# Slot weights as one-hot products in fp32r, weight split in two parts on the moving side

## Chip, cores and metric

The kernel runs on one core of a Trainium2 chip. The metric is the device time in microseconds (us) of one execution; lower is better. The time of the kernel before is the median of three runs.

## What is computed

One transformer layer over 512 latent tokens (two token mixers, a merge, then a PEER feed-forward part and a final norm). Only the PEER part matters here. For each token and each of 8 heads, 16 of 128 x 128 = 16384 single-neuron experts are chosen, so a token has 128 slots, each with an expert number and a softmax weight:

```python
idx = (jnp.take_along_axis(i1, ci // PEER_TOPK, axis=-1) * N_KEYS
       + jnp.take_along_axis(i2, ci % PEER_TOPK, axis=-1)).reshape(PEER_BLOCK, -1)
g = jax.nn.softmax(sc, axis=-1).reshape(PEER_BLOCK, -1)
act = jax.nn.gelu(jnp.einsum("med,md->me", u[idx], hb), approximate=False)
return jnp.einsum("me,med->md", (g * act).astype(hb.dtype), v[idx])
```

The kernel does not gather. It computes the activation of all 16384 experts for all tokens, and needs beside it a dense matrix W(i, j) per token: the sum of the weights of the slots whose expert is (i, j). With the 128 slots of a token on the partitions, W is a product of two one-hot matrices, one for i and one for j, with the weight multiplied into one of them.

## The kernel before

The part after the merge has three phases. `phase_route` chooses the experts. `phase_weights` builds W for 512 tokens and stores it to DRAM. `phase_experts` reads it back, multiplies it with the activations and forms the output. Through all three runs `Hidden`, the product of the expert matrix u with the tokens, in 128 tiles of 128 experts. Each tile is 8 times `product`: three fp32r matmuls of a 128x128 stationary operand and 512 moving columns (high*high, low*high, high*low; L85, L86, L87), 24 matmuls in all. ScalarE applies gelu to the tile (L1889) and splits the high part of a coming u tile (L1869, `Hidden.split`); then `Hidden.rest` (L1873) subtracts it to get the low part, on GpSimd in the route phase and on VectorE in the weights phase; SyncE loads u and stores activations.

`phase_weights` is the phase that the change touches. It has 64 steps (16 loop bodies with 4 steps). In each step every engine does one tile of `Hidden` and two groups of four tokens (`SUB = 4`). A group uses one of four buffers (`S = 4`), so a buffer is used again two steps later. The order on the engines within step q is fixed by the program:

- TensorE: the 24 matmuls of the tile, then for each of the two groups the wait for its operands and four fp32 matmuls `ps_w <- oi, oj` (L2368), stationary operand `oi` (128x128), 128 moving columns of `oj`. I call these two groups the slot section of the step, s the first and s' the second.
- VectorE: for each of the two groups, `oi` of tokens 0 and 1 (two tensor_scalar, is_equal and times weight, L2322) and `oj` of all four tokens (one tensor_tensor with both inputs broadcast, L2324); then `Hidden.rest` of the step. What it builds in step q+1 is what TensorE uses in step q+1, so these operations stand behind `rest` of step q.
- ScalarE: gelu, split, and for each group `away` = |i - iota| (L2377), the evacuation of `ps_w` to `w_block` (L2400) and `oi` of token 2 as relu(w - w*away) (L2381), one turn ahead.
- GpSimd: for each group a small copy (L2343) and `oi` of token 3 (L2349).

`slots` holds for all tokens i, j, weight, -i and -weight; it is written at the end of `phase_route` (L2236 to L2240). After every 64 tokens SyncE stores 4 MB of W to DRAM (L2306).

Of the kernel before, what the change touches and what calls it, by code (L numbers as in the profile page):

```python
# [13 lines left out]
F32R = mybir.dt.float32r  # L14
U32 = mybir.dt.uint32
ALU = mybir.AluOpType
ACT = mybir.ActivationFunctionType
AX = mybir.AxisListType

P = 128  # L20
D = 1024
KT = D // P
TX, TC = 512, 256
# [19 lines left out]
PH, NK, TOPK = 8, 128, 16  # L43
# [1858 lines left out]
def phase_route(nc, a, b, hidden):  # L1902


    with ExitStack() as ctx:
        sb = alloc(nc, ctx)

        def sem(name):
# [7 lines left out]
        S = b.acc[:, 4:8].rearrange("p (h k) (t n) -> p h k t n", h=2, n=NK)  # L1916
# [12 lines left out]
        iota = sb("iota16", [P, TOPK])  # L1929
        src = sb("slot_src", [P, 2, TT, PH, TOPK])  # L1930
        SC = sb("SC", [P, TT, PH, TOPK])
        weight = sb("slot_weight", [P, TT, PH * TOPK])
        total = sb("soft_total", [P, TT * PH])
        ps_q = [ctx.enter_context(nc.psum_tensor(f"ps_q{k}", [P, TX], F32)) for k in range(2)]
        ps_s = [ctx.enter_context(nc.psum_tensor(f"ps_sc{k}", [P, TT, NK], F32)) for k in range(2)]
        keys_in, iota_in = sem("rt_keys"), sem("rt_iota")
# [13 lines left out]
        turn, turn_g = sem("rt_turn"), sem("rt_turn_pool")  # L1950
        sub_done, exp_done, soft, weight_done, turned, slots_out = (
            sem(f"sl_{n}") for n in ("sub", "exp", "dve", "weight", "turned", "out"))
# [167 lines left out]
        def _(v):  # L2120
# [12 lines left out]
            with v.Fori(0, PH // 2) as i:  # L2133
                for hh in range(2):
# [3 lines left out]
                    for t, p in both:  # L2138
                        m = v.max(top[:, hh, t, p, 0:8], S[:, hh, p, t, :])
                    dve_s.mark(m)  # L2140
                for hh in range(2):
                    when(i, f"max1{hh}")
                    for t, p in both:
                        m = v.max_index(ix[:, hh, t, p, 0:8], top[:, hh, t, p, 0:8], S[:, hh, p, t, :])
                    dve_s.mark(m)
                    for t, p in both:
                        m = v.match_replace(left[:, hh, t, p], top[:, hh, t, p, 0:8], S[:, hh, p, t, :], LOW)
                    dve_s.mark(m)
                for hh in range(2):
                    when(i, f"left{hh}", s_free[hh])  # L2150
                    for t, p in both:
                        m = v.max(top[:, hh, t, p, 8:16], left[:, hh, t, p])
                    dve_s.mark(m)
                for hh in range(2):
                    when(i, f"max2{hh}")
                    for t, p in both:
                        m = v.max_index(ix[:, hh, t, p, 8:16], top[:, hh, t, p, 8:16], left[:, hh, t, p])
                    dve_s.mark(m)

                    for t in range(TT):  # L2160
                        m = v.tensor_tensor(cand[:, hh, t], top[:, hh, t, 0, :].unsqueeze(2).to_broadcast([P, TOPK, TOPK]),
                                            top[:, hh, t, 1, :].unsqueeze(1).to_broadcast([P, TOPK, TOPK]), ALU.add)
                    dve_s.mark(m)
                flat = cand[:].rearrange("p h t a c -> p h t (a c)")
                for hh in range(2):
                    when(i, f"cand{hh}")
                    for t in range(TT):
                        m = v.max(ctop[:, hh, t, 0:8], flat[:, hh, t])
# [60 lines left out]
            link = Count(v, soft)  # L2229
# [5 lines left out]
            for k in range(3):  # L2235
                v.wait_ge(turned, k + 1)  # L2236
                bank = ps_q[k][:] if k < 2 else ps_s[0][:].rearrange("p t n -> p (t n)")
                v.tensor_copy(b.slots[:, k, 0:TX], bank).then_inc(slots_out, 1)
                if k != 1:
                    v.tensor_scalar(b.slots[:, 3 + k // 2, 0:TX], bank, -1.0, None, ALU.mult).then_inc(slots_out, 1)  # L2240


W_TOKENS = 64
# [3 lines left out]
def phase_weights(nc, a, b, hidden, w_dram):  # L2247
# [6 lines left out]
    with ExitStack() as ctx:  # L2254
        sb = alloc(nc, ctx)

        def sem(name):
            return b.semaphore(nc, name)


        oi = b.acc[:, 0:S].rearrange("p s (k n) -> p s k n", n=NK)
        oj = b.acc[:, S:2 * S].rearrange("p s (k n) -> p s k n", n=NK)
        iota = sb("iota128", [P, NK])[:]
        away = sb("w_away", [P, S, NK])
        cur = sb("w_token", [P, S, 2])
        wb = sb("w_block", [P, 2, NK, W_TOKENS])
        ps = [ctx.enter_context(nc.psum_tensor(f"ps_w{k}", [P, SUB, NK], F32)) for k in range(S)]
        small_in = sem("w_in")
        built, built_a, mm, evac = ([sem(f"w_{n}{k}") for k in range(S)] for n in ("built", "built_act", "mm", "evac"))
        dist = sem("w_dist")  # L2270
        built_p, fetched, turn = sem("w_built_pool"), sem("w_fetched"), sem("w_turn")
        stored = [sem(f"w_stored{k}") for k in range(2)]
        block = ctx.enter_context(nc.Block())
        n_outer = W_BLOCKS // 2
# [37 lines left out]
        @block.vector  # L2312
        def _(v):
            v.wait_ge(small_in, 16)

            def body(t0, n, half, g, o):
                for q in range(steps):
                    for s, r, dt in subs(q):

                        v.wait_ge(mm[s], n * TURNS + (r + 1))  # L2320
                        for k in range(SUB - 2):
                            v.tensor_scalar(oi[:, s, k], iota, b.slots[:, 0, bass.ds(t0 + (dt + k), 1)],  # L2322
                                            b.slots[:, 2, bass.ds(t0 + (dt + k), 1)], ALU.is_equal, ALU.mult)
                        v.tensor_tensor(oj[:, s], iota.unsqueeze(1).to_broadcast([P, SUB, NK]),  # L2324
                                        b.slots[:, 1, bass.ds(t0 + dt, SUB)].unsqueeze(2).to_broadcast([P, SUB, NK]),
                                        ALU.is_equal).then_inc(built[s], 1)
                    hidden.rest(v, n + (ROUTE_T + 1), q)

            bodies(v, body)

        @block.gpsimd
        def _(g_):

            g_.wait_ge(small_in, 16)
            g_.sem_inc(built_p, S)

            def body(t0, n, half, g, o):
                for q in range(steps):
                    for s, r, dt in subs(q):

                        g_.wait_ge(built_p, n * (TURNS * S) + (r * S + s + 1))
                        g_.sem_inc(turn, 1)
                        g_.tensor_copy(cur[:, s], b.slots[:, 0:3:2, bass.ds(t0 + (dt + SUB - 1), 1)].rearrange(  # L2343
                            "p k o -> p (k o)")).then_inc(fetched, 1)
                        g_.wait_ge(fetched, n * (TURNS * S) + (r * S + s + 1))

                        g_.wait_ge(mm[s], n * TURNS + (r + 1))
                        g_.sem_inc(turn, 1)
                        g_.tensor_scalar(oi[:, s, SUB - 1], iota, cur[:, s, 0:1], cur[:, s, 1:2],  # L2349
                                         ALU.is_equal, ALU.mult).then_inc(built_p, 1)  # L2350

            bodies(g_, body)

        @block.tensor
        def _(pe):
            for s in range(S):
                pe.sem_inc(mm[s], 1)

            def body(t0, n, half, g, o):
                for q in range(steps):  # L2360
                    hidden.multiply(pe, n + ROUTE_T, q)
                    for s, r, dt in subs(q):
                        pe.wait_ge(built[s], n * TURNS + (r + 1))
                        pe.wait_ge(built_a[s], n * TURNS + (r + 1))
                        pe.wait_ge(built_p, n * (TURNS * S) + (r * S + s + S + 1))
                        pe.wait_ge(evac[s], n * TURNS + (r + 1))
                        for k in range(SUB):
                            m = pe.matmul(ps[s][:, k, :], oi[:, s, k], oj[:, s, k], start=True, stop=True)  # L2368
                        m.then_inc(mm[s], 1)

            bodies(pe, body)

        @block.scalar
        def _(act):

            def measure(t, s):
                act.activation(away[:, s], iota, ACT.Abs, bias=b.slots[:, 3, bass.ds(t, 1)]).then_inc(dist, 1)  # L2377

            def build(t, s, turn_):
                act.wait_ge(dist, turn_ * S + (s + 1))  # L2380
                act.activation(oi[:, s, SUB - 2], away[:, s], ACT.Relu, bias=b.slots[:, 2, bass.ds(t, 1)],  # L2381
                               scale=b.slots[:, 4, bass.ds(t, 1)]).then_inc(built_a[s], 1)

            act.wait_ge(small_in, 16)
            for s in range(S):
                act.sem_inc(evac[s], 1)
                measure(s * SUB + (SUB - 2), s)
                build(s * SUB + (SUB - 2), s, 0)

            def body(t0, n, half, g, o):  # L2390
                for q in range(steps):
                    hidden.gelu(act, n + ROUTE_T, q)
                    hidden.split(act, n + (ROUTE_T + 1), q)
                    for s, r, dt in subs(q):
                        t_next = t0 + (S * SUB + dt + SUB - 2)
                        measure(t_next, s)
                        act.wait_ge(mm[s], n * TURNS + (r + 2))

                        act.wait_ge(stored[half], o * 16 + 16)
                        act.activation(wb[:, half, :, bass.ds(g * BODY + dt, SUB)].rearrange("p j t -> p t j"),  # L2400
                                       ps[s][:], ACT.Copy).then_inc(evac[s], 1)
                        build(t_next, s, n * TURNS + (r + 1))

            bodies(act, body)


# [183 lines left out]
def build_program(nc, a, out):  # L2590
    with ExitStack() as ctx:
# [67 lines left out]
        with ExitStack() as route:  # L2659
            st = alloc(nc, route)  # L2660

            b.slots = st("slots", [P, 5, TX + 16])
            phase_route(nc, a, b, hidden)
            phase_weights(nc, a, b, hidden, w_dram)
        b.clear_semaphores(nc)
# [92 lines left out]
```

## Time and profile before

| | us |
|---|---|
| median of 3 runs | 2840.35 (2839.32 to 2850.03) |
| the profiled execution | 2841.56 |
| its span, first to last instruction | 2839.3 |
| TensorE busy, whole span | 2548.7 (90%) |
| route phase's last 100 us, TensorE busy | 68.9 of 100 |
| weights phase, 1420 to 1886, TensorE busy | 464.1 of 466 |
| the same stretch, VectorE, ScalarE, GpSimd busy | 221.8, 297.2, 238.3 |
| from 1950 to the end, TensorE busy | 875.4 of 889 |

The page gives each engine's busy share; the table cuts the span at the phases, since the phases have different limits. A matmul's duration in the trace holds its way through the array, so matmuls overlap, and the pace is read from start to start.

### The profile page before, as it was taken

The numbers are of one execution on the slowest core, as the hardware profiler recorded it, in microseconds if no ns is written. First come the engines' busy times: TensorE is split into PE (matmuls) and PEld (weight loads), VectorE is DVE, ScalarE is ACT, GpSimd is POOL, SyncE is SP. The second block draws the span as 40 slices with busy tenths as digits, with TensorE's granted clock in tenths as the row PEclk, the third lists the DMA queues.
The fourth block names the chain that finished last, engine by engine and source line by source line (L and its number), as shares of the span: only waits on it lengthen the run. The fifth ranks groups of instructions, "written<-read, shape, count | busy, mean of one in ns | idle before, by whom it ended". The sixth has DMA issues, their size and how long they took to land. (4 is left out here: it accounts for less than half of the span.)

```text
span 2839.3 us, 53307 instructions
## 1 busy us (share of the span) xinstructions
PE 2548.7 (90%) x19772; PEld 2098.7 (74%) x19772; DVE 1327.9 (47%) x2679; ACT 1026.1 (36%) x1763; POOL 767.5 (27%) x627
## 2 busy tenths in 40 slices
PE   5998839759995997899599999979999999999998
PEld 2884429559983875788488888868888888888886
DVE  4764345465554232499744444420014444444443
ACT  3322433423333222332266666642223222222222
POOL 1520013124422342554455555524420000000000
PEclk9999759979997998999799999989999999999999
DMA  5551000000003221422335444554436555555551
GB/s 226 184 170 37 1 8 1 9 2 0 0 5 111 88 97 33 160 92 82 107 141 184 167 169 182 214 200 145 144 118 234 188 198 187 201 184 203 182 204 60
DMA packets 164052, 349.10 MB, mean 123 GB/s; under 512 B 13512, under 2 KB 79560, under 8 KB 161936
## 3 DMA queue, kind: packets, MB, share of 16 engines
q1 hardware_dynamic: 163984, 348.19, 35.2%
q8 instruction: 44, 0.72, 0.1%
q14 instruction: 24, 0.20, 0.0%
HBM read 276.84 MB, written 71.30 MB: 123 GB/s over the span
## 5 line engine op out<-in xcount | busy, mean ns | idle before, releaser
L85 PE MATMUL ps_a<-h_hi,u_hi 128*128 128x512 f32 x1024 | 407.3, 398 | 23.5 <-PEq L105 16.5
L2537 DVE TENSOR_TENSOR v_lo<-v_raw,v_hi 128x1024 fp32r<-128x1024 f32 x128 | 158.2, 1236 | 564.9 <-ACT v_hi L2495 564.9
L86 PE MATMUL ps_a<-h_hi,u_lo 128*128 128x512 f32 x1024 | 401.1, 392 | 0.0
L87 PE MATMUL ps_a<-h_lo,u_hi 128*128 128x512 f32 x1024 | 400.9, 391 | 0.0
L2495 ACT ACTIVATE v_hi<-v_raw 128x1024 fp32r<-128x1024 f32 x128 | 135.8, 1061 | 477.7 <-PE ps_a L87 469.3
L85 PE MATMUL ps_y<-gated_hi,v_hi 128*128 128x512 f32 x768 | 299.5, 390 | 3.1 <-DVE gated_lo L2539 3.1
L86 PE MATMUL ps_y<-gated_hi,v_lo 128*128 128x512 f32 x768 | 299.5, 390 | 0.0
L87 PE MATMUL ps_y<-gated_lo,v_hi 128*128 128x512 f32 x768 | 299.3, 390 | 0.0
L85 PEld LDWEIGHTS ps_a<-h_hi,u_hi 128*128 128x128 f32 x1024 | 194.3, 190 | 62.6 <-issue 23.1
L87 PEld LDWEIGHTS ps_a<-h_lo,u_hi 128*128 128x128 f32 x1024 | 193.6, 189 | 40.8
L1889 ACT ACTIVATE act<-ps_a 128x512 f32<-128x512 f32 x128 | 76.4, 597 | 407.6 <-PE ps_a L87 407.6
L86 PEld LDWEIGHTS ps_a<-h_hi,u_lo 128*128 128x128 f32 x1024 | 194.0, 189 | 38.0
L2349 POOL TENSOR_SCALAR mixed<-iota,w_token 128x128 f32<-128x128 f32 x128 | 149.5, 1168 | 213.3 <-PE ps_w L2368 197.8
L1873 POOL TENSOR_TENSOR u_lo<-u_raw,u_hi 128x1024 fp32r<-128x1024 f32 x64 | 154.8, 2422 | 188.7 <-ACT u_hi L1869 188.7
L1873 DVE TENSOR_TENSOR u_lo<-u_raw,u_hi 128x1024 fp32r<-128x1024 f32 x64 | 78.4, 1225 | 242.4 <-ACT u_hi L1869 242.4
L85 PEld LDWEIGHTS ps_y<-gated_hi,v_hi 128*128 128x128 f32 x768 | 144.5, 188 | 33.6 <-DVE v_lo L2537 3.5
L86 PEld LDWEIGHTS ps_y<-gated_hi,v_lo 128*128 128x128 f32 x768 | 144.6, 188 | 30.1
L87 PEld LDWEIGHTS ps_y<-gated_lo,v_hi 128*128 128x128 f32 x768 | 144.5, 188 | 30.1
L1869 ACT ACTIVATE u_hi<-u_raw 128x1024 fp32r<-128x1024 f32 x128 | 134.4, 1051 | 57.4 <-DMA u_raw<-in_uT 57.4
L2400 ACT ACTIVATE w_block<-ps_w 128x512 f32 x128 | 141.2, 1103 | 0.0
L1681 POOL TENSOR_TENSOR mg_w_lo<-mg_raw,mg_w_hi 128x1024 fp32r<-128x1024 f32 x36 | 87.7, 2437 | 196.7 <-ACT mg_w_hi L1730 196.7
L2368 PEld LDWEIGHTS ps_w<-mixed 128*128 128x128 f32 x1024 | 124.1, 191 | 5.0
(497 smaller groups left out, 5314.9 us busy)
## 6 DMA issues: line engine op xcount, KB each, us to landing
u_raw<-in_uT SPq DMA_DIRECT2D x128, 512.0 KB, 3.5
v_raw<-in_v SPq DMA_DIRECT2D x128, 512.0 KB, 4.9
a_scratch<-act SPq DMA_DIRECT2D x128, 256.0 KB, 2.2
w_scratch<-w_block SPq DMA_DIRECT2D x8, 4096.0 KB, 12.0
w_ring<-w_scratch SPq DMA_DIRECT2D x64, 512.0 KB, 4.5
gated<-a_scratch SPq DMA_DIRECT2D x128, 256.0 KB, 4.9
mg_raw<-in_w_merge SPq DMA_DIRECT2D x36, 512.0 KB, 3.4
vM<-in_ada_rows SPq DMA_DIRECT2D x32, 512.0 KB, 4.7
```

Of the source, the lines that this page charges most:

```text
L85: pe.matmul(out, wh, xh, start=first, stop=False)
L86: pe.matmul(out, wl, xh, start=False, stop=False)
L87: return pe.matmul(out, wh, xl, start=False, stop=last)
L1681: g.tensor_tensor(wl[:, k], raw[:, k], wh[:, k], ALU.subtract).then_inc(w_lo, 1)
L1869: act.activation(self.uh[:, q], self.raw[:, q % 2], ACT.Copy).then_inc(self.hi, 1)
L1873: eng.tensor_tensor(self.ul[:, q], self.raw[:, q % 2], self.uh[:, q], ALU.subtract).then_inc(self.lo, 1)
L1889: act.activation(self.act[:, q % 2], self.ps[q % 2][:], ACT.Gelu).then_inc(self.out, 1)
L2349: g_.tensor_scalar(oi[:, s, SUB - 1], iota, cur[:, s, 0:1], cur[:, s, 1:2], ALU.is_equal, ALU.mult).then_inc(built_p, 1)
L2368: m = pe.matmul(ps[s][:, k, :], oi[:, s, k], oj[:, s, k], start=True, stop=True)
L2400: act.activation(wb[:, half, :, bass.ds(g * BODY + dt, SUB)].rearrange("p j t -> p t j"), ps[s][:], ACT.Copy).then_inc(evac[s], 1)
L2495: act.activation(vh[:, q], v_raw[:, q], ACT.Copy).then_inc(v_hi, 1)
L2537: v.tensor_tensor(vl[:, q], v_raw[:, q], vh[:, q], ALU.subtract).then_inc(v_lo, 1)
```

## The change

In `phase_weights` all operands become fp32r. The weight is split in two fp32r parts, high and low (w = high + low), and multiplied into the j side, which is the moving one: `oh` = high * onehot(j), `ol` = low * onehot(j). The i side is a plain one-hot `oi`. A token is now two matmuls into the same PSUM columns instead of one: `oi` with `oh`, then `oi` with `ol`. Each operand is built for four tokens in one operation: VectorE writes `mark` = onehot(j) and `oi` (is_equal) and `oh` = mark * high; GpSimd writes `ol` = mark * low. The building on ScalarE and the small copies on GpSimd are gone. In `phase_route`, `slots` gets the rows i, j, high and low instead of five rows.

```diff
-                v.tensor_copy(b.slots[:, k, 0:TX], bank).then_inc(slots_out, 1)
-                if k != 1:
-                    v.tensor_scalar(b.slots[:, 3 + k // 2, 0:TX], bank, -1.0, None, ALU.mult).then_inc(slots_out, 1)
+                if k < 2:
+                    v.tensor_copy(b.slots[:, k, 0:TX], bank).then_inc(slots_out, 1)
+                else:
+                    link(v.tensor_scalar(w_high[:], bank, 1.0, None, ALU.mult))
+                    v.tensor_copy(b.slots[:, 2, 0:TX], w_high[:]).then_inc(slots_out, 1)
+                    v.tensor_tensor(b.slots[:, 3, 0:TX], bank, w_high[:], ALU.subtract).then_inc(slots_out, 1)
...
+            def spread(row, t):
+                return b.slots[:, row, bass.ds(t, SUB)].unsqueeze(2).to_broadcast([P, SUB, NK])
+
+            line = iota.unsqueeze(1).to_broadcast([P, SUB, NK])
...
+                        v.wait_ge(built_p[s], n * TURNS + (r + 1))
+                        v.tensor_tensor(mark[:, s], line, spread(1, t0 + dt), ALU.is_equal).then_inc(marked[s], 1)
                         v.wait_ge(mm[s], n * TURNS + (r + 1))
-                        for k in range(SUB - 2):
-                            v.tensor_scalar(oi[:, s, k], iota, b.slots[:, 0, bass.ds(t0 + (dt + k), 1)],
-                                            b.slots[:, 2, bass.ds(t0 + (dt + k), 1)], ALU.is_equal, ALU.mult)
-                        v.tensor_tensor(oj[:, s], iota.unsqueeze(1).to_broadcast([P, SUB, NK]),
-                                        b.slots[:, 1, bass.ds(t0 + dt, SUB)].unsqueeze(2).to_broadcast([P, SUB, NK]),
-                                        ALU.is_equal).then_inc(built[s], 1)
+                        v.tensor_tensor(oi[:, s], line, spread(0, t0 + dt), ALU.is_equal)
+                        v.wait_ge(marked[s], n * TURNS + (r + 1))
+                        v.tensor_tensor(oh[:, s], mark[:, s], spread(2, t0 + dt), ALU.mult).then_inc(built[s], 1)
                     hidden.rest(v, n + (ROUTE_T + 1), q)
...
-                        g_.tensor_copy(cur[:, s], b.slots[:, 0:3:2, bass.ds(t0 + (dt + SUB - 1), 1)].rearrange(
-                            "p k o -> p (k o)")).then_inc(fetched, 1)
...
-                        g_.tensor_scalar(oi[:, s, SUB - 1], iota, cur[:, s, 0:1], cur[:, s, 1:2],
-                                         ALU.is_equal, ALU.mult).then_inc(built_p, 1)
+                        g_.wait_ge(marked[s], n * TURNS + (r + 1))
                         g_.wait_ge(mm[s], n * TURNS + (r + 1))
+                        g_.tensor_tensor(ol[:, s], mark[:, s],
+                                         b.slots[:, 3, bass.ds(t0 + dt, SUB)].unsqueeze(2).to_broadcast([P, SUB, NK]),
+                                         ALU.mult).then_inc(built_p[s], 1)
...
                         for k in range(SUB):
-                            m = pe.matmul(ps[s][:, k, :], oi[:, s, k], oj[:, s, k], start=True, stop=True)
+                            pe.matmul(ps[s][:, k, :], oi[:, s, k], oh[:, s, k], start=True, stop=False)
+                            m = pe.matmul(ps[s][:, k, :], oi[:, s, k], ol[:, s, k], start=False, stop=True)
                         m.then_inc(mm[s], 1)
...
-                        t_next = t0 + (S * SUB + dt + SUB - 2)
-                        measure(t_next, s)
                         act.wait_ge(mm[s], n * TURNS + (r + 2))
...
-                        build(t_next, s, n * TURNS + (r + 1))
```

## Rows read from the trace of the kernel before

**Rows 1.** Busy time by stretch of all engines, then granted clock and DMA.
```profile
1420.00:1886.00 466.00, 464.14 (x2557) 403.02 (x2555) 221.76 (x448) 297.15 (x519) 238.26 (x256) 1.00 0.47 170
```

**Rows 2.** Groups by line, 1420 to 1886: busy, mean ns, idle before and releaser.
```profile
L2368 PE MATMUL ps_w<-mixed 128*128 128x128 f32 x1024 | 124.5, 275 | 0.0
L1873 DVE TENSOR_TENSOR u_lo<-u_raw,u_hi 128x1024 fp32r<-128x1024 f32 x64 | 78.4, 1225 | 242.4 <-ACT u_hi L1869 242.4
```

**Rows 3.** Timeline of one step: start, length (us), engine; x16 counts merged instructions.
```profile
1599.84 1.95 PE L2368 MATMUL ps_w<-mixed 128*128 128x128 f32 x16
...
1600.13 0.60 ACT L1889 ACTIVATE act<-ps_a 128x512 f32<-128x512 f32 x1 [2.72 <-PE ps_a L87]
...
1601.54 0.48 PE L85 MATMUL ps_a<-h_hi,u_hi 128*128 128x512 f32 x1
...
1601.70 1.23 DVE L1873 TENSOR_TENSOR u_lo<-u_raw,u_hi 128x1024 fp32r<-128x1024 f32 x1 [3.88 <-ACT u_hi L1869]
...
1602.84 0.60 DVE L2322 TENSOR_SCALAR mixed<-iota,slots 128x128 f32<-128x128 f32 x2
...
1603.21 1.59 POOL L2349 TENSOR_SCALAR mixed<-iota,w_token 128x128 f32<-128x128 f32 x1 [0.23 <-POOL w_token L2343]
...
1603.36 0.69 DVE L2324 TENSOR_TENSOR mixed<-iota,slots 128x512 f32<-128x512 f32 x1
...
1603.96 0.60 DVE L2322 TENSOR_SCALAR mixed<-iota,slots 128x128 f32<-128x128 f32 x2
...
1607.08 1.95 PE L2368 MATMUL ps_w<-mixed 128*128 128x128 f32 x16
...
1608.78 0.48 PE L85 MATMUL ps_a<-h_hi,u_hi 128*128 128x512 f32 x1
...
1608.85 1.22 DVE L1873 TENSOR_TENSOR u_lo<-u_raw,u_hi 128x1024 fp32r<-128x1024 f32 x1 [3.69 <-ACT u_hi L1869]
```

**Rows 4.** Weight loads (PEld), timeline and groups: 128 stationary columns, fp32, fp32r, transposes.
```profile
53.79 2.75 PEld L369 LDWEIGHTS ps_pc<-ident,fC 2*128 2x128 f32 x24 [1.61 <-ACT fC L267]
264.39 1.57 PEld L1202 LDWEIGHTS ps_gt<-gate_ident,gate_turn 36*128 36x128 f32 x24 [0.76 <-issue]
L2368 PEld LDWEIGHTS ps_w<-mixed 128*128 128x128 f32 x1024 | 124.1, 191 | 5.0
L85 PEld LDWEIGHTS ps_a<-h_hi,u_hi 128*128 128x128 f32 x1024 | 194.3, 190 | 62.6 <-issue 23.1
```

**Rows 5.** Timeline of fp32r matmuls with 256 moving columns, start to start.
```profile
150.49 0.28 PE L85 MATMUL ps_pc<-h_hi,win_hi 128*128 128x256 f32 x1
...
152.76 0.28 PE L87 MATMUL ps_pc<-h_lo,win_hi 128*128 128x256 f32 x1
```

**Rows 6.** Timeline where VectorE and GpSimd both run two-input operations.
```profile
363.11 2.48 POOL L1374 TENSOR_TENSOR mixed<-ml_hc,ml_ssq 128x512 f32<-128x512 f32 x2
363.25 1.44 DVE L1606 TENSOR_TENSOR mixed<-mixed 128x512 f32<-128x512 f32 x1 [1.00 <-POOL mixed L1374]
364.62 1.52 DVE L1603 TENSOR_TENSOR mixed<-ml_hc,ml_ssq 128x512 f32<-128x512 f32 x1
365.55 1.48 POOL L1374 TENSOR_TENSOR mixed<-ml_hc,ml_ssq 128x512 f32<-128x512 f32 x1
```

**Rows 7.** One line's instructions: ns min/median/max, then GpSimd groups of other sizes.
```profile
L1374 POOL TENSOR_TENSOR mixed<-ml_hc,ml_ssq x4: 1033/1482/1541, 361.6 to 365.6; 128x512 f32<-128x512 f32 x4
L1873 POOL TENSOR_TENSOR u_lo<-u_raw,u_hi 128x1024 fp32r<-128x1024 f32 x64 | 154.8, 2422 | 188.7 <-ACT u_hi L1869 188.7
L755 POOL TENSOR_TENSOR ks_x<-ke,ginv_x 128x256 f32<-128x256 f32 x16 | 11.6, 727 | 3.8 <-POOL qs_x L755 3.8
```

**Rows 8.** Timelines of the end of the route phase and of the weights phase.
```profile
1413.44 2.34 POOL L1873 TENSOR_TENSOR u_lo<-u_raw,u_hi 128x1024 fp32r<-128x1024 f32 x1 [3.05 <-ACT u_hi L1869]
1882.89 1.05 ACT L1869 ACTIVATE u_hi<-u_raw 128x1024 fp32r<-128x1024 f32 x1
1886.88 0.33 SPq L2306 DMA_DIRECT2D w_scratch<-w_block  x1
```

More of the change, by code:

```diff
@@ L1933, in phase_route @@
         total = sb("soft_total", [P, TT * PH])
+        w_high = sb("weight_hi", [P, TX], F32R)
         ps_q = [ctx.enter_context(nc.psum_tensor(f"ps_q{k}", [P, TX], F32)) for k in range(2)]
@@ L2258, in sem @@
             return b.semaphore(nc, name)
-        oi = b.acc[:, 0:S].rearrange("p s (k n) -> p s k n", n=NK)
-        oj = b.acc[:, S:2 * S].rearrange("p s (k n) -> p s k n", n=NK)
+        mark = b.acc[:, 0:S].rearrange("p s (k n) -> p s k n", n=NK)
+        oi, oh, ol = (sb(n, [P, S, SUB, NK], F32R) for n in ("one_i", "one_j_hi", "one_j_lo"))
         iota = sb("iota128", [P, NK])[:]
-        away = sb("w_away", [P, S, NK])
-        cur = sb("w_token", [P, S, 2])
         wb = sb("w_block", [P, 2, NK, W_TOKENS])
@@ L2268, in phase_weights @@
         small_in = sem("w_in")
-        built, built_a, mm, evac = ([sem(f"w_{n}{k}") for k in range(S)] for n in ("built", "built_act", "mm", "evac"))
-        dist = sem("w_dist")
-        built_p, fetched, turn = sem("w_built_pool"), sem("w_fetched"), sem("w_turn")
+        marked, built, built_p, mm, evac = ([sem(f"w_{n}{k}") for k in range(S)]
+                                            for n in ("marked", "built", "built_pool", "mm", "evac"))
         stored = [sem(f"w_stored{k}") for k in range(2)]
@@ L2332, in _ @@
         def _(g_):
-            g_.wait_ge(small_in, 16)
-            g_.sem_inc(built_p, S)
+            for s in range(S):
+                g_.sem_inc(built_p[s], 1)
             def body(t0, n, half, g, o):
@@ L2339, in body @@
                     for s, r, dt in subs(q):
-                        g_.wait_ge(built_p, n * (TURNS * S) + (r * S + s + 1))
-                        g_.sem_inc(turn, 1)
-                        g_.tensor_copy(cur[:, s], b.slots[:, 0:3:2, bass.ds(t0 + (dt + SUB - 1), 1)].rearrange(
-                            "p k o -> p (k o)")).then_inc(fetched, 1)
-                        g_.wait_ge(fetched, n * (TURNS * S) + (r * S + s + 1))
+                        g_.wait_ge(marked[s], n * TURNS + (r + 1))
                         g_.wait_ge(mm[s], n * TURNS + (r + 1))
-                        g_.sem_inc(turn, 1)
-                        g_.tensor_scalar(oi[:, s, SUB - 1], iota, cur[:, s, 0:1], cur[:, s, 1:2],
-                                         ALU.is_equal, ALU.mult).then_inc(built_p, 1)
+                        g_.tensor_tensor(ol[:, s], mark[:, s],
+                                         b.slots[:, 3, bass.ds(t0 + dt, SUB)].unsqueeze(2).to_broadcast([P, SUB, NK]),
+                                         ALU.mult).then_inc(built_p[s], 1)
             bodies(g_, body)
@@ L2363, in body @@
                         pe.wait_ge(built[s], n * TURNS + (r + 1))
-                        pe.wait_ge(built_a[s], n * TURNS + (r + 1))
-                        pe.wait_ge(built_p, n * (TURNS * S) + (r * S + s + S + 1))
+                        pe.wait_ge(built_p[s], n * TURNS + (r + 2))
                         pe.wait_ge(evac[s], n * TURNS + (r + 1))
                         for k in range(SUB):
-                            m = pe.matmul(ps[s][:, k, :], oi[:, s, k], oj[:, s, k], start=True, stop=True)
+                            pe.matmul(ps[s][:, k, :], oi[:, s, k], oh[:, s, k], start=True, stop=False)
+                            m = pe.matmul(ps[s][:, k, :], oi[:, s, k], ol[:, s, k], start=False, stop=True)
                         m.then_inc(mm[s], 1)
@@ L2374, in _ @@
         def _(act):
[L2376 to L2384, printed above, removed]
             for s in range(S):
                 act.sem_inc(evac[s], 1)
-                measure(s * SUB + (SUB - 2), s)
-                build(s * SUB + (SUB - 2), s, 0)
             def body(t0, n, half, g, o):
@@ L2660, in build_program @@
             st = alloc(nc, route)
-            b.slots = st("slots", [P, 5, TX + 16])
+            b.slots = st("slots", [P, 4, TX + 16])
             phase_route(nc, a, b, hidden)
```

## The prediction

> **What bounds the kernel now.** I read first the busy time cut by stretch, then the groups by line within the weights phase, then the timeline of one step. In the weights phase TensorE is busy 464.1 of 466 us at the full clock, and no other engine is over 64% [rows 1]. So this phase is bound by TensorE alone, and the reader should see that ScalarE, VectorE and GpSimd have slack. The slot matmuls start behind no idle time at all [rows 2]. In the timeline a slot section starts at 1599.84 and the next one at 1607.08: a step takes 7.24 us, and 64 of them are 463 us. Of these the slot section is 1607.08 to 1608.78, 1.70 us, and the tile of `Hidden` from 1601.54 to 1607.08, 5.54 us [rows 3]. Eight fp32 matmuls show as 16 records, so a record takes 106 ns.
>
> **What the change does to TensorE.** It takes away 16 records of fp32 (8 tokens) and puts 16 fp32r matmuls there (8 tokens, 2 each). The trace shows no fp32r matmul with 128 moving columns. Two bounds: fp32r with 256 columns goes from 150.49 to 152.76 in 20 steps from start to start, 113.5 ns each [rows 5], so the stream alone should need about half, 57 ns for 128 columns. But each matmul also loads 128 columns of weights. With only 2 moving columns, the 24 loads of L369 take 2.75 us: (2.75 - 0.19) / 23 = 111 ns from load to load; there the stream is nothing, so the load sets the pace. That is fp32. The load of an fp32r operand is 190 ns long in the trace, that of an fp32 operand 191 ns, whereas the transposes of L1202 have loads at (1.57 - 0.14) / 23 = 62 ns [rows 4]. So fp32r loads look like fp32 loads, not like those of the transposes. The two products of a token use the same `oi`, but the program gives each matmul its own load; I find no load left out in this trace. I take 16 x 107 = 1.71 us for the new slot section: TensorE gains nothing. Ends: 16 x 62 = 0.99 us below, and above 16 x 113 = 1.81 us (the pace of rows 5), or 3.40 us if a short fp32r matmul should pass four times like fp32.
>
> The Trainium skill (TensorE: Matmul & The Clock Gate, section LDWEIGHTS) gives a load as columns / 1.2, an estimate of 107 ns for 128 columns; rows 4 agree. The same page (section Back-to-back issue gap) gives about 81 ns for a load and matmul pair with 128 columns, and it says the fast weight load is off for FP32; by 81 ns the section would be an estimated 1.30 us. No row shows that pace with these operands; it is a rival below.
>
> **What it does to VectorE and GpSimd.** VectorE had per step four tensor_scalar (0.60 us a pair) and two tensor_tensor of 128x512, and `rest` [rows 3]. It now has six tensor_tensor of 128x512 with two SBUF inputs, 0.60 us from start to start, 0.68 from start to end (L2324 is just this form). 6 x 0.60 + 1.14 = 4.7 us of 7.24: enough room by count. GpSimd had a copy and a 128x128 operation, and now has one two-input operation of 128x512 per group. The nearest row is L1374, same size and same kind of broadcast: 1033 ns when alone. The other GpSimd operations of 256 and 1024 elements (727 and 2422 ns) would give 1.28 us for 512 [rows 7].
>
> The count is not enough, because of two things. First, where these operations stand. VectorE builds the operands of step q+1 behind `rest` of step q, and `rest` waits for ScalarE's split, which follows gelu, which follows the tile. With T the start of a slot section, `rest` starts at T+1.86 (1601.70 - 1599.84), and at T+1.77 in the next step (1608.85 - 1607.08), mean 1.81, and the next VectorE operation 1.14 later, at T+2.95 [rows 3]. Second, two-input operations of the two engines do not overlap. L1606 starts at 363.25 and takes 1.44 us in place of 0.69; it ends 0.58 us after the GpSimd operation (363.11 + 1.00 = 364.11) has ended. The GpSimd operation that waits meanwhile ends at 365.55, 0.9 us after L1606 at 364.69, and L1603 ends 0.59 after that, at 366.14 [rows 6]. They take turns, 0.9 us for GpSimd, 0.59 for VectorE. In the weights phase itself L2349 takes 1.59 us instead of 0.79 beside L2324 [rows 3].
>
> The Trainium skill (GPSIMD Engine Reference, section Specifications) says the same of the design: the SBUF interfaces are shared with VectorE, with contention for VectorE instructions with two SBUF inputs. It speaks against this change, and the trace agrees (1.44 us for 0.69).
>
> So from T, in the order of the queues: mark 2.95, oi 3.55 to 4.23; GpSimd's ol (waiting since mark ended at 3.63) to 5.13; oh to 5.72; mark' from 5.64, oi' 6.24 to 6.92; ol' to 7.82; oh' to 8.41. TensorE can start s' about 0.15 later (semaphore, and a load that isn't ahead), at T+8.56. With the old step it needs s' at T + 7.24 + 0.85 = T+8.09. It comes 0.47 us late. The group s is ready at 5.72, long before 7.24. Behind s' stand its matmuls, 0.85, and the next tile, 5.54, so the loop is T(q+2) = T(q) + 8.56 + 0.85 + 5.54 = 14.95 us, 7.475 per step instead of 7.24. The sum: 64 x 0.235 = +15.0 us. If GpSimd took turns in another order, the sum of the port's occupation is the same, so I take this as robust against the order. With the 1.28 us form GpSimd is 0.38 longer, twice in two steps: another 64 x 0.38 = +24 us. With a pace of 113 ns on TensorE: +0.05 per step, +3.
>
> **What it does elsewhere.** ScalarE loses away and build; it had slack (297 of 466) [rows 1], gelu and split come before them in its order, so this gives nothing in a step. At the end of the phase the last evacuation no longer stands behind one build and two measures. The split ends at 1883.94, two evacuations of about 1.1 would end at 1886.2, and the store that now starts at 1886.88 [rows 8] starts 0.7 us earlier: -0.7 us, since the next phase waits for the store. At the end of the route phase VectorE has three operations instead of two behind the last transpose, some 0.5 us more; it would end near 1414, and GpSimd's L1873 ends at 1415.78 in the same block [rows 8], which covers it. Without this cover it would cost 0.5. The waits that VectorE gets: for `built_p` of two steps ago, for `mm` of two steps ago, for `marked`, its own mark that ended during oi. The first two are fulfilled long before; behind the waiting instruction `rest` is queued, whose slack is T(q+1)+1.81 - (T(q)+8.41), over 0.8 us. SyncE's loads follow `rest`, as before. The phase of the experts is untouched.
>
> The sum is +15.0 - 0.7 = +14.3 on the profiled 2841.56, which is 1.2 over the median; on the median it is 2854.7, I say 2855.
>
> **Rivals.**
> 1. Contention does not bite (the engines share less than rows 6 show, or `ol` gets its turn in a gap). Then s' is ready at 2.95 + 5 x 0.60 + 0.68 = T+6.63, in time, and TensorE sets the step at 7.24 to 7.34: 2840 to 2846, not slower. For: VectorE's operations in rows 3 aren't longer beside GpSimd's. Against: rows 6. It decides as soon as s' comes before T+8.09.
> 2. The slot section shrinks to 0.99 us (loads like the transposes'). TensorE's step would be 6.53. With contention the loop is 8.56 + 0.49 + 5.54 = 14.59, 7.30 a step: +4, 2844, same. The chain eats the gain.
> 3. The same without contention: 64 x (6.53 - 7.24) = -45, 2795, faster. By the page's 81 ns it would be an estimated -26 us. This needs two things against the rows.
> 4. Short fp32r matmuls pass four times: section 3.40, step 8.94, +109 us, 2949. For: nothing under 256 columns is in the trace. Against: the 256-column ones pass once.
> That the change doesn't do what it says, that is, TensorE's slot section stays at 1.7 us, is part of my forecast and of rival 1.
>
> **How the numbers follow.** Chances: forecast 0.55 (2846 to 2880, 0.34 of it above 0.5%, as the unknown costs, GpSimd's above all, point upwards), rival 1 0.22, rival 2 0.06, rival 3 0.09, rival 4 0.08. A measurement can tell about 0.5% (14 us) from no change. Slower: 0.34 + 0.08 = 0.42. Same: 0.21 + 0.22 + 0.06 = 0.49. Faster: 0.09. The range leaves out rivals 3 and 4 and takes in GpSimd's upper bound: 2838 to 2880. The forecast's own range is 2846 to 2880.
>
> **What the profile after would show.** Slot section: 16 PE records of about 107 ns, 1.7 us; 62 ns would be rivals 2 and 3, 212 ns rival 4. VectorE: oh and oh' of about 1.5 us instead of 0.69, each beside a GpSimd operation; all at 0.69 would be rival 1. TensorE idle before s' of about 0.5 us every other step or 0.24 in each, with GpSimd or VectorE as the releaser; the step at 7.47. The forecast would be wrong if `rest` or the split move, if GpSimd takes another time than 0.9 to 1.3 us, or if the port is shared otherwise.

## The result and the profile after

The changed kernel takes 2853.24 us (median of 12 runs, 2849.54 to 2863.01), the kernel before beside it 2839.84 us (12 runs). The ratio is 1.0044, 95% interval 1.0029 to 1.0059: slower by 0.44%, which is 12.5 us (the two medians lie 13.4 us apart), clear of the noise, but under the 0.5% that I had set as the border between same and slower. The forecast was 2855.

Whole spans of single executions are a bad measure here. The profiled executions differ by 8.7 us (2839.3 and 2848.0), but in the one of after the weights phase already starts 5.2 us sooner (the load of iota is issued at 1411.62 instead of 1416.83), before any changed work. So I measure in the phase itself. The mean step is the distance from the first to the last slot section by 63:

| | first section | last section | mean step | iota load to first load of the next phase | rest |
|---|---|---|---|---|---|
| before | 1426.08 | 1882.20 | 7.240 | 483.5 | 939.0 |
| after | 1420.75 | 1890.84 | 7.462 | 497.7 | 938.7 |

The phase is 14.3 us longer, of which the steps are 63 x 0.222 = 14.0. The next phase takes the same time to 0.3 us. This step of after answers to [rows 3]; the columns are start, length, engine:

```profile
1601.64 2.06 ACT L2385 ACTIVATE w_block<-ps_w 128x512 f32 x2
1601.78 1.23 DVE L1873 TENSOR_TENSOR u_lo<-u_raw,u_hi 128x1024 fp32r<-128x1024 f32 x1 [1.21 <-ACT u_hi L1869]
1602.92 0.69 DVE L2327 TENSOR_TENSOR mixed<-iota,slots 128x512 f32<-128x512 f32 x1
...
1603.52 0.69 DVE L2329 TENSOR_TENSOR one_i<-iota,slots 128x512 fp32r<-128x512 f32 x1
1603.79 1.32 POOL L2346 TENSOR_TENSOR one_j_lo<-mixed,slots 128x512 fp32r<-128x512 f32 x1 [3.76 <-DVE mixed L2327]
1604.12 1.53 DVE L2331 TENSOR_TENSOR one_j_hi<-mixed,slots 128x512 fp32r<-128x512 f32 x1
1605.58 0.68 DVE L2327 TENSOR_TENSOR mixed<-iota,slots 128x512 f32<-128x512 f32 x1
1606.18 0.68 DVE L2329 TENSOR_TENSOR one_i<-iota,slots 128x512 fp32r<-128x512 f32 x1
1606.44 1.33 POOL L2346 TENSOR_TENSOR one_j_lo<-mixed,slots 128x512 fp32r<-128x512 f32 x1 [1.33 <-DVE mixed L2327]
1606.79 1.52 DVE L2331 TENSOR_TENSOR one_j_hi<-mixed,slots 128x512 fp32r<-128x512 f32 x1
...
1607.20 0.22 PE L2365 MATMUL ps_w<-one_j_hi,one_i 128*128 128x128 f32 x1
...
1607.37 0.27 PE L2365 MATMUL ps_w<-one_j_hi,one_i 128*128 128x128 f32 x1
...
1607.48 0.27 PE L2366 MATMUL ps_w<-one_j_lo,one_i 128*128 128x128 f32 x1
...
1608.37 0.33 PE L2365 MATMUL ps_w<-one_j_hi,one_i 128*128 128x128 f32 x1 [0.16 <-DVE one_j_hi L2331]
...
1614.82 0.22 PE L2365 MATMUL ps_w<-one_j_hi,one_i 128*128 128x128 f32 x1
```

Read it from the top: VectorE's subtraction (u_lo), then mark (its tile shares a buffer that the profile calls `mixed`), one_i, and then one_j_hi with 1.53 us where the same size takes 0.69 two lines above. It ends at 1605.65, 0.54 us after GpSimd's operation (1605.11), and the GpSimd operation takes 1.32 us because it stands still until one_i is through at 1604.21 and then needs 0.90. The same happens in the second group, whose one_j_hi ends at 1608.31; 0.06 later TensorE starts the group's first matmul, which had to wait. The slot section started at 1607.20, the next one at 1614.82: 7.62 us. The step before it took 7.29 (1599.91 to 1607.20). Late and timely steps alternate, 14.91 us for this pair, 14.92 in the mean. The groups by line over the phase show that this holds for all of them (idle before, and its releaser, at the end):

```profile
L2331 DVE TENSOR_TENSOR one_j_hi<-mixed,slots 128x512 fp32r<-128x512 f32 x127 | 193.9, 1527 | 0.0
L2327 DVE TENSOR_TENSOR mixed<-iota,slots 128x512 f32<-128x512 f32 x126 | 85.9, 682 | 0.0
L2329 DVE TENSOR_TENSOR one_i<-iota,slots 128x512 fp32r<-128x512 f32 x126 | 85.9, 682 | 0.0
L1873 DVE TENSOR_TENSOR u_lo<-u_raw,u_hi 128x1024 fp32r<-128x1024 f32 x64 | 78.4, 1225 | 60.8 <-ACT u_hi L1869 60.8
```

VectorE's idle time before u_lo fell from 242.4 us [rows 2] to 60.8. And TensorE waits for it, which it never did before; from the waits between 1430 and 1890 (total, times, longest):

```profile
PEld ps_w L2365 <- DVE one_j_hi L2331: 8.7, 30, 0.3
PE ps_w L2365 <- DVE one_j_hi L2331: 2.2, 14, 0.2
```

Thirty waits of the weight load, one in every other step. The 14 waits of the matmuls lie in the same delays, so the two sums are not to be added. What the lateness costs is read from the steps: the timely ones take 7.287 us, and over the phase the late ones bring the mean to 7.462, 63 x 0.175 = 11.0 us.

The other 3 us are in every step, 7.287 against 7.240. They are not in the pace of the matmuls. After, a matmul starts 111 ns behind the one before it (1607.37, 1607.48). Before, 16 records of 275 ns [rows 2] last 1.95 us together [rows 3], so they start (1.95 - 0.275) / 15 = 112 ns apart: the fp32 section already had 16 loads (1024 in 64 steps, [rows 4]) and the pace of a load. What differs is its edges:

```profile
1601.54 0.28 PE L2366 MATMUL ps_w<-one_j_lo,one_i 128*128 128x128 f32 x1
...
1601.65 0.45 PE L85 MATMUL ps_a<-h_hi,u_hi 128*128 128x512 f32 x1
...
1607.20 0.22 PE L2365 MATMUL ps_w<-one_j_hi,one_i 128*128 128x128 f32 x1
1607.26 0.28 PE L2366 MATMUL ps_w<-one_j_lo,one_i 128*128 128x128 f32 x1
```

Behind the last slot matmul the tile now starts 0.11 us later, before it was 0.03; the second matmul of a section comes 0.06 behind the first (1607.20, 1607.26), before it was 0.11; and the tile itself is 0.01 longer. That is 0.08 - 0.05 + 0.01, the 0.047 within rounding. Why the edges differ is not shown by any run.

### The profile page after: what moved, and what is told of

It is laid out like the page before. It is cut to its first block and busy times, and to the rows that moved or that the text cites. A ratio compares the mean times of both kernels' runs of the same rounds, so it can differ in the third digit from the quotient of the medians.

```text
span 2848.0 us, 52006 instructions
## 1 busy us (share of the span) xinstructions
PE 2554.1 (90%) x19772; PEld 2100.8 (74%) x19772; DVE 1521.7 (53%) x2679; ACT 951.3 (33%) x1499; POOL 698.9 (25%) x499
## 5 line engine op out<-in xcount | busy, mean ns | idle before, releaser
L2346 POOL TENSOR_TENSOR one_j_lo<-mixed,slots 128x512 fp32r<-128x512 f32 x128 | 167.8, 1311 | 313.1 <-DVE mixed L2327 313.1
L2331 DVE TENSOR_TENSOR one_j_hi<-mixed,slots 128x512 fp32r<-128x512 f32 x128 | 195.4, 1527 | 0.0
L2385 ACT ACTIVATE w_block<-ps_w 128x512 f32 x128 | 131.1, 1138 | 0.0
L2365 PE MATMUL ps_w<-one_j_hi,one_i 128*128 128x128 f32 x512 | 117.5, 270 | 4.8 <-DVE one_j_hi L2331 2.3
```

Of the source, the lines that this page charges most:

```text
L2331: v.tensor_tensor(oh[:, s], mark[:, s], spread(2, t0 + dt), ALU.mult).then_inc(built[s], 1)
L2346: g_.tensor_tensor(ol[:, s], mark[:, s], b.slots[:, 3, bass.ds(t0 + dt, SUB)].unsqueeze(2).to_broadcast([P, SUB, NK]), ALU.mult).then_inc( ...
L2365: pe.matmul(ps[s][:, k, :], oi[:, s, k], oh[:, s, k], start=True, stop=False)
```

## The experiments

The theory: (a) an fp32r matmul of 128 columns takes as long as its weight load, so TensorE gains nothing; (b) VectorE operations with two SBUF inputs and GpSimd's take turns; (c) this makes the second group late because its operands are built behind the subtraction that waits for ScalarE. The first four runs take (b) and (a) apart, the later ones (c), and whether a cheaper load pays. For each run I give the step, measured as in the table, since only this is free of what happens in the earlier stages.

### GpSimd idle in the steps

```diff
             for s in range(S):
                 g_.sem_inc(built_p[s], 1)
+                g_.tensor_scalar(ol[:, s], iota.unsqueeze(1).to_broadcast([P, SUB, NK]), 0.0, None,
+                                 ALU.mult).then_inc(built_p[s], 1)
...
-                        v.wait_ge(built_p[s], n * TURNS + (r + 1))
...
-                        pe.wait_ge(built_p[s], n * TURNS + (r + 2))
+                        pe.wait_ge(built_p[s], 2)
```

> The changed kernel, but GpSimd makes the low operand once, as zeros, ahead of the loop, and is idle in the steps (so the low part of the weight is left out of W). TensorE still does both matmuls of a token. Theory (VectorE and GpSimd take turns at the SBUF interface, and this makes the second group late): oh falls from 1.53 to 0.69 us, the second group comes in time, the step falls from 7.46 us to TensorE's own 5.54 + 16 x 0.111 = 7.3 us, 64 x 0.15 = 10 us under the changed kernel: 2843 us, still some 4 us over the kernel before. Rival (the second group is late because VectorE alone has too much between the split and the slot section): the step stays at 7.46 us, 2853 us. Rival (GpSimd's result is late by itself, not through sharing): 2843 too, but oh stays as long as it is.

Measured: step 7.287 us; 2841.70 us median (10 runs), ratio to before 1.0012 (0.9993 to 1.0031). In this kernel's trace, one line's instructions (min/median/max ns):

```profile
L2330 DVE TENSOR_TENSOR one_j_hi<-mixed,slots x128: 675/682/1093, 1428.7 to 1890.2; 128x512 fp32r<-128x512 f32 x128
```

The low part is left out of W here. The operation is back at 682 ns, the lateness is gone, and 0.175 of the 0.222 us go with it. VectorE has the same six operations, so its own load is not what made the group late. This run alone doesn't tell sharing from a late result of GpSimd, except by the 682 ns.

### iota and the high part read from PSUM

```diff
-            line = iota.unsqueeze(1).to_broadcast([P, SUB, NK])
+            v.tensor_copy(iota_p[:], iota).then_inc(put, 1)
+            v.tensor_copy(high_p[:], b.slots[:, 2, 0:TX]).then_inc(put, 1)
+            v.wait_ge(put, 2)
+            line = iota_p[:].unsqueeze(1).to_broadcast([P, SUB, NK])
...
-                        v.tensor_tensor(oh[:, s], mark[:, s], spread(2, t0 + dt), ALU.mult).then_inc(built[s], 1)
+                        v.tensor_tensor(oh[:, s], mark[:, s], high_p[:, bass.ds(t0 + dt, SUB)].unsqueeze(2).to_broadcast([P, SUB, NK]), ALU.mult).then_inc(built[s], 1)
```

> The changed kernel with the whole computation, but iota and the high part of the weight are copied to two PSUM banks ahead of the loop and read from there, so that mark, oi and oh each have one SBUF input and one PSUM input. GpSimd works as before. Theory (it is two SBUF inputs of a VectorE operation that collide with GpSimd): oh is 0.69 us although GpSimd's operation of 1.0 to 1.2 us runs beside it, the step is 7.3 us, 2843 us. Rival (any VectorE operation is held while GpSimd works, whatever its inputs): oh stays at 1.5 us, the step at 7.46 us, 2853 us.

Measured: step 7.287 us; 2840.19 us median (10 runs), ratio 0.9998 (0.9982 to 1.0014). Timeline of one group, and the line of GpSimd's operation:

```profile
1602.33 0.68 DVE L2335 TENSOR_TENSOR one_i<-ps_iota,slots 128x512 fp32r<-128x512 f32 x1
...
1602.59 1.04 POOL L2352 TENSOR_TENSOR one_j_lo<-mixed,slots 128x512 fp32r<-128x512 f32 x1 [4.54 <-DVE mixed L2333]
...
1602.93 0.68 DVE L2337 TENSOR_TENSOR one_j_hi<-mixed,ps_high 128x512 fp32r<-128x512 f32 x1
```

```profile
L2352 POOL TENSOR_TENSOR one_j_lo<-mixed,slots x128: 1039/1041/1044, 1420.0 to 1881.3; 128x512 fp32r<-128x512 f32 x128
```

All work is done, GpSimd's operation runs beside VectorE's, and now each takes its own time: 1041 ns in place of 1324, 0.68 us in place of 1.53. Nothing but the place of one input of mark, one_i and one_j_hi was changed. That settles (b): it is the second SBUF input that collides. It also gives back the 11 us of the lateness, with fp32r and all; the step stays 0.047 us over that of the kernel before, which the whole time can't resolve.

### Half the stream, and half the load

```diff
-                            m = pe.matmul(ps[s][:, k, :], oi[:, s, k], ol[:, s, k], start=False, stop=True)
+                            m = pe.matmul(ps[s][:, k, 0:64], oi[:, s, k], ol[:, s, k, 0:64], start=False, stop=True)
```

> The changed kernel, but the matmul with the low part streams only 64 of its 128 moving columns (the low part of the weight is left out of W for j from 64 on). The loads are unchanged. Theory (each fp32r matmul here takes as long as its load of 128 stationary columns): all matmuls still start 111 ns apart. Rival (the stream and a fixed cost for each matmul set the pace): a matmul behind a half one starts some 27 ns sooner, 84 ns, and the slot section falls from 1.78 to about 1.56 us.

and, in another kernel, the other way round:

```diff
-                            pe.matmul(ps[s][:, k, :], oi[:, s, k], oh[:, s, k], start=True, stop=False)
-                            m = pe.matmul(ps[s][:, k, :], oi[:, s, k], ol[:, s, k], start=False, stop=True)
+                            pe.matmul(ps[s][:, k, :], oi[:, s, k], oh[:, s, k], start=True, stop=True)
+                            m = pe.matmul(ps[s][0:64, k, :], oi[:, s, k, 0:64], ol[:, s, k], start=True, stop=True)
```

> The changed kernel, but the matmul with the low part loads only 64 of the 128 stationary columns and writes only 64 rows, as a product of its own (so W holds the low part alone for i under 64 and the high part alone above). Its stream is the full 128 columns. Theory (load sets the pace): the pair of a token takes 111 + 56 = 167 ns in place of 222, the slot section 1.33 us in place of 1.78; the step is then held by VectorE and GpSimd at about (8.4 + 0.15 + 0.67 + 5.54) / 2 = 7.4 us, so that the whole time falls by only 4 to 5 us. Rival (a fixed 111 ns for each matmul): the pair stays at 222 ns.

Both leave a part of the weight out of W and are for reading the pace alone. Timeline of the half stream (128x64 moving):

```profile
1605.82 0.30 PE L2365 MATMUL ps_w<-one_j_hi,one_i 128*128 128x128 f32 x1
1605.96 0.24 PE L2366 MATMUL ps_w<-one_j_lo,one_i 128*128 128x64 f32 x1
1606.05 0.30 PE L2365 MATMUL ps_w<-one_j_hi,one_i 128*128 128x128 f32 x1
```

and of the half load (128*64 stationary):

```profile
1602.45 0.28 PE L2365 MATMUL ps_w<-one_j_hi,one_i 128*128 128x128 f32 x1
1602.56 0.22 PE L2366 MATMUL ps_w<-one_j_lo,one_i 128*64 128x128 f32 x1
1602.62 0.28 PE L2365 MATMUL ps_w<-one_j_hi,one_i 128*128 128x128 f32 x1
```

With half the stream a pair still takes 0.23 us in these rows and 0.224 over the section (the starts within it shift, the pair doesn't: expected 0.222, by the rival 0.195). With half the load it takes 0.17, as expected. So (a) holds: the load sets the pace. The steps were 7.465 and 7.363 us in the mean, from one profiled execution each. The first is that of the changed kernel. The second is lower by 0.10, although a timely step, which TensorE alone sets, fell by 0.44 (from 7.287 to 6.847): VectorE and GpSimd hold the loop now, as I had worked out (7.4). A cheaper slot section alone is mostly lost.

### Operands built one step earlier

```diff
+            build(0, 0, 0)
+
             def body(t0, n, half, g, o):
                 for q in range(steps):
...
+                    if q < steps - 1:
+                        build(t0, n, q + 1)
+                    else:
+                        build(t0 + BODY, n + 1, 0)
```

`build(t0, n, q)` is the old loop over the two groups of step q, word for word; `hidden.rest` of step q now stands behind it.

> The changed kernel, but VectorE builds the operands of step q+1 before it does the u_lo subtraction of step q instead of behind it (the operands of step 0 are built ahead of the loop, and one set too many at the end). Theory (the lateness needs both: the turns at the SBUF interface, and the place behind the subtraction that waits for ScalarE's split): oh stays at 1.53 us, VectorE is busy 6.8 us a step, which fits in 7.3; the second group is early, and the step falls to TensorE's 7.3 us: 2843 us. Rival (sharing alone costs the time, as VectorE's sum of work or through another engine): the step stays at 7.46 us, 2853 us.

Measured: step 7.287 us; the phase, measured as in the table, is 485.9 us against 497.7 with the change. The whole time says less: the ratio to before is 1.0014 (0.9992 to 1.0036), while the medians, 2852.62 us (10 runs) and 2841.02, lie 0.4% apart; more on this below. The line of one_j_hi:

```profile
L2329 DVE TENSOR_TENSOR one_j_hi<-mixed,slots x130: 681/1526/1534, 1430.0 to 1892.3; 128x512 fp32r<-128x512 f32 x130
```

The engines still take turns, 1526 ns, and the step is free of it. So (c) holds: sharing costs nothing by itself, it costs where a late engine waits behind a subtraction.

### The same with bf16 operands

A one-hot is exact in bf16. The weight is split into two 2-byte parts in place of two 4-byte ones, so fewer of its bits are kept: this is not quite the same computation.

```diff
-        oi, oh, ol = (sb(n, [P, S, SUB, NK], F32R) for n in ("one_i", "one_j_hi", "one_j_lo"))
+        oi, oh, ol = (sb(n, [P, S, SUB, NK], mybir.dt.bfloat16) for n in ("one_i", "one_j_hi", "one_j_lo"))
...
-        w_high = sb("weight_hi", [P, TX], F32R)
+        w_high = sb("weight_hi", [P, TX], mybir.dt.bfloat16)
```

In the changed kernel as it is:

> The changed kernel with bf16 instead of fp32r operands, and the two-input VectorE operations as they are. Theory (VectorE and GpSimd in turns hold the second group): TensorE's section falls to 1.0 us, but the loop is (8.4 + 0.15 + 0.5 + 5.54) / 2 = 7.3 us a step, so the time is 2842 us, some 50 us over e5_bf16_psum although TensorE has the same work. Rival (the section sets the step also here): 2791 us.

with the PSUM inputs:

> e2_psum with the one-hot operands and the two parts of the weight in bf16 instead of fp32r (a one-hot is exact in bf16; the weight keeps 16 bits instead of 22). Theory (the load of 4-byte stationary columns costs 107 ns, and a 2-byte load costs less): the matmuls start 56 to 62 ns apart, the slot section is 1.0 us, TensorE's step 6.5 us; without sharing the second group is ready at T+6.8, so the loop is (6.8 + 0.5 + 5.54) / 2 = 6.4 us and TensorE decides: 64 x (6.5 - 7.24) = -47 us, 2791 us. Rival (a load costs 107 ns whatever the type): section 1.78 us, 2840 us.

and with the operands one step earlier, without PSUM:

> e7_early with bf16 instead of fp32r operands: VectorE and GpSimd still take turns (all VectorE operations have two SBUF inputs), but the operands are built one step ahead. Theory: VectorE's work is 6 x 0.60 + 1.14 + 2 x 0.85 = 6.45 us a step, TensorE's 5.54 + 0.9 = 6.44, so the step is 6.45 to 6.6 us, and the time some 2790 to 2800 us. This tells apart place and sharing for the bf16 operands: with the sharing but behind the subtraction (e6_bf16) the step was 7.27 us. Rival (sharing holds the loop also when the operands are early): the step stays over 7 us.

| bf16 operands | step, expected | step, measured | time, ratio to before |
|---|---|---|---|
| as the change has it | 7.3 | 7.309 | one run |
| iota and high part from PSUM | 6.5 | 6.501 | 2797.15 us, 0.984 (0.9808 to 0.9872) |
| operands one step earlier | 6.45 to 6.6 | 6.447 | 2790.65 us, 0.9835 (0.9805 to 0.9866) |

In the second of them, a load (PEld) and the pace of the matmuls, to hold against [rows 4]:

```profile
L2371 PEld LDWEIGHTS ps_w<-one_j_hi,one_i x512: 96/98/98, 1420.0 to 1830.3; 128*128 128x128 bf16 x171
```

```profile
1504.39 0.22 PE L2371 MATMUL ps_w<-one_j_hi,one_i 128*128 128x128 bf16 x1
1504.44 0.22 PE L2372 MATMUL ps_w<-one_j_lo,one_i 128*128 128x128 bf16 x1
1504.50 0.22 PE L2371 MATMUL ps_w<-one_j_hi,one_i 128*128 128x128 bf16 x1
```

A load is 98 ns long in place of 192, and the matmuls start 56 ns apart in place of 111. Whether the load or the stream sets these 56 ns is not told by these runs. The slot section is 0.9 us. In the kernel with the change's own order little of this arrives (7.309 in place of 7.462), because TensorE waits up to 1.6 us for the second group:

```profile
PEld ps_w L2365 <- DVE one_j_hi L2331: 43.2, 28, 1.6
```

Once either remedy is in, both new kernels beat the kernel before by 1.6%. The two can't be told apart by their intervals. In the traces they differ: with the operands one step earlier every step is 6.447 us, while with the PSUM inputs every fourth one, the last of a loop body, is 0.09 to 0.62 us longer, 3.4 us in all. What holds these is not shown, and no run has both remedies at once.

The Trainium skill (TensorE: Matmul & The Clock Gate, section Weight-path perf modes) says that the fast weight load is on for 128 weights of a type that isn't FP32. These runs agree, and show that fp32r counts as FP32 there: 192 ns a load and 111 ns a matmul, against 98 and 56 in bf16. The 81 ns for a load and matmul pair with 128 columns, which the Trainium skill gives on the same page (section Back-to-back issue gap), are met by neither.

## Why the prediction was right, and where it wasn't

**TensorE gains nothing.** That was right, and the price of 16 x 107 was not. The 106 ns of an fp32 record came from dividing the section, 1.70 us, by 16; from start to start these records were already 112 ns apart, as the 111 of rows 4 and the 111 measured after. Both sections are 16 loads long, so the pace of the load costs nothing against before. The term "+3 at a pace of 113" meets the 3.0 us that every step lost (63 x 0.047; 7.287 us in three kernels) by luck: these are at the edges of the section, for which the prediction had no term. By its own loop 6 ns more for the 8 matmuls of the late group are also 0.05 us in two steps, not in one, so +1.5 and not +3.

**The turns.** I had 0.9 us for GpSimd and 0.59 for VectorE, oh ready at T+5.72 and oh' at T+8.41. In the trace, with T = 1599.91, they end at 1605.65 and 1608.31: T+5.74 and T+8.40. The 0.15 us from there to the group's first matmul came from no row; it measures 0.06, and the rest of the loop 6.45 (1608.37 to 1614.82) in place of 6.39, which offset each other in part. TensorE was 0.33 us late, not 0.47 (0.44 from 1607.93 to 1608.37, less the 0.11 of a load), since the group was due later than by the old step. The loop was worked out as 14.95 us for two steps and measures 14.91; the mean step 7.475 and 7.462. In time the lateness is 63 x (7.462 - 7.287) = 11.0 us. My sum had 15.0 for it, on a base of 7.24 instead of 7.29; with the 3.0 of the edges the steps lost 14.0.

**The nearest row carried it.** The size and the kind of broadcast of the GpSimd operation were those of L1374 [rows 7], 1033 ns alone. It is 1041 ns alone with the fp32r output. The line through other sizes, 1.28 us, would have given 24 us more.

**The end of the phase.** Here a term was wrong: -0.7 us. From the last slot section to the first load of the next phase it was 18.09 us before and is 18.50 after. The last evacuation does end sooner after its section (the store is issued 4.08 us behind the section's start instead of 4.68), but the store takes longer to be through, 14.42 us to the next load instead of 13.41. Now it is issued 0.91 us behind a 512 KB load of u, and was 1.51 behind. All variants with the new section show 14.1 to 14.6 us. That the two transfers share the queues and that this takes the gain back is likely, but no run tried it.

**The sum** was +14.3 and is +12.5 by the ratio, +13.4 by the medians, +14.3 by the phase itself. That the last agrees to the tenth is luck: 15.0 for the steps was 1.0 too much, and -0.7 for the end 1.1 too little (the start of the phase is 0.1 shorter). The forecast point lay just above the border between same and slower, 0.5%, and the chances leaned to same (0.49 against 0.42); the measured 0.44% is just below it.

**Rivals.** No contention (0.22): not so, but e2_psum shows what it would have been, 2840. A load like a transpose's (0.06, 0.09) and four passes (0.08): both excluded by 111 ns. The rival with a small section and contention was worth 7.30 a step; e6_bf16 is just this, 7.31 a step.

## What to carry to other kernels

Before GpSimd is given a share of elementwise work, look at whether VectorE's operations at that moment have two SBUF inputs: if so, add the two durations instead of overlapping them, or move one input to PSUM. A short matmul costs at least its weight load, 111 ns here, and an fp32 matmul shows as two loads, so two fp32r matmuls of 128 columns are no cheaper than one in fp32; with both operands in bf16 they were, at 56 ns each. When a pace is read from a trace, take it from start to start and not from a section's length by its number of matmuls: the edges were 3 us here. And before an engine's work is made cheaper, follow the operand chain to see what is late next: here 0.85 us a step were to be had on TensorE, and most of it was lost until the operands came earlier or VectorE stopped sharing.

## What was not expected of the hardware

One and the same stage, long before the changed code, takes a different time from one execution to the next. The matmuls ahead of it end at about 280 us in all kernels, but the stage behind it starts 10 to 12 or 27 us later in some of them. Granted clock between 281 and 300 us (third number from the end), first in the kernel before, then in the bf16 kernel with the change's own order:

```profile
281.00:300.00 19.00, 15.11 (x58) 7.35 (x60) 6.13 (x15) 3.42 (x12) 0.43 (x1) 0.82 0.06 16
```

```profile
281.00:300.00 19.00, 15.08 (x41) 7.68 (x42) 5.09 (x13) 2.28 (x8) 0.00 (x0) 0.51 0.04 13
```

0.82 is a mix of the two levels, 0.51 is nearly all the lower one (1.2 GHz), in a stage whose instructions are the same (58 and 41 matmuls of it fall into the stretch). Why the clock stays low in some executions is not shown. In the second kernel the weights phase starts at 1440.45, in the kernel before at 1416.83; that is why its one time, 2869.55 us, says nothing about its step of 7.31 us. The times of the early-operands kernel fall into two groups, 2840 to 2843 and 2852 to 2856; its profiled execution, 2852.35, has a clock of 0.58 in this stretch. That the clock parts the others too is likely, but they have no trace. With such a stage in a kernel, a change of 0.5% is better read from the length of its own phase than from the total.
